# Paced weight loads and a reordered last stretch of a recurrence chain in a two-layer hybrid decoder trunk

## The reference

```python
def token_mixer(h, w_in, ...):
    p = h @ w_in
    p_r, p_m, p_g = jnp.split(p, [RWKV_COLS, RWKV_COLS + MLSTM_COLS], axis=-1)
    y_r = rwkv7_branch(p_r, ...) @ branch_w_rwkv
    y_m = mlstm_branch(p_m, ...) @ branch_w_mlstm
    g_r, g_m = jnp.split(jax.nn.sigmoid(p_g), 2, axis=-1)
    return (g_r * y_r + g_m * y_m) @ w_out

def rwkv7_recurrence(r, w, k, v, a, b):      # per head, state s is 64x64
    def step(s, inp):
        sa = einsum('bhvk,bhk->bhv', s, a_t)
        s = s * w_t + sa * b_t + v_t * k_t
        return s, einsum('bhvk,bhk->bhv', s, r_t)
```

## Time and profile before

| | |
|---|---|
| three runs | 1408.48, 1412.29, 1412.35 us (median 1412.29) |
| the profiled execution's own time | 1416.23 us |
| its span | 1414.5 us |
| TensorE matmul busy | 1383.9 us, 98% of the span |
| mean granted TensorE clock | 0.995 |
| chain of the first layer | about 376 to 453 us from the span's start |
| chain of the second layer | about 1060 to 1140 us |

### The profile page before, as it was taken

The page is one execution under the profiler, slowest core; times in us unless marked ns, Lnnn a source line. Parts: engine busy times, 40 slices in busy tenths (PEclk is TensorE's granted clock), DMA queues, the critical chain, the costliest instruction groups (busy, mean ns, idle before and its releaser), DMA issues.

```text
span 1414.5 us, 31209 instructions
## 1 busy us (share of the span) xinstructions
PE 1383.9 (98%) x13824; PEld 1314.8 (93%) x13824; DVE 1078.2 (76%) x1838; ACT 288.4 (20%) x566; POOL 67.9 (5%) x137
## 2 busy tenths in 40 slices
PE   7999999999999999999999999999998999999998
PEld 3999999888988999999999999988898889999998
DVE  5899889788765769887888886787976575856665
ACT  2211101442231031110031110035231302211101
POOL 5110000000000000100000000000000000000000
PEclk9999999999999999999999999999999999999999
DMA  9999786443423758887768886454442337456530
GB/s 347 323 329 325 285 308 178 141 134 105 115 71 119 238 180 277 278 292 295 254 193 268 280 275 227 157 161 143 120 116 72 116 125 263 134 195 209 191 137 31
DMA packets 214054, 283.16 MB, mean 200 GB/s; under 512 B 13288, under 2 KB 177504, under 8 KB 213920
## 3 DMA queue, kind: packets, MB, share of 16 engines
q1 hardware_dynamic: 194976, 211.11, 46.2%
q0 software_dynamic: 17952, 69.21, 13.8%
q10 hardware_dynamic: 992, 0.85, 0.2%
HBM read 280.10 MB, written 1.05 MB: 199 GB/s over the span
## 4 chain that ended last, share of the span: by engine, by line
PE 94%; DVE 4%; issue 1%; DMA 1%; POOL 0%; ACT 0%; ACTq 0%; POOLq 0%; DVEq 0%
PE ps L1899 92%; PE ps L1903 1%; DMA ada_stage<-in_ada_w_dram 1%; DVE ada_acc L1050 1%; PE ps L2413 0%; DVE ada_turn L1056 0%; DVE ada_red L1057 0%; DVE arena L1279 0%; DVE stat L1332 0%; DVE stat L1326 0%; DVE xn L1329 0%; DVE arena L1330 0%; DVE xn L1339 0%; DVE arena L1282 0%; DVE arena L1280 0%
## 5 line engine op out<-in xcount | busy, mean ns | idle before, releaser
L1899 PE MATMUL ps<-hT,ring 128*128 128x128 f32 (+2 forms) x2352 | 341.9, 302 | 1.7 <-ACT hT L702 1.3
L1899 PEld LDWEIGHTS ps<-hT,ring 128*128 128x128 f32 (+1 forms) x2352 | 313.4, 191 | 26.0 <-issue 8.3
L1899 PE MATMUL ps<-y_both,arena 128*128 128x128 f32 x2304 | 266.6, 275 | 1.0 <-issue 1.0
L1899 PEld LDWEIGHTS ps<-y_both,arena 128*128 128x128 f32 x2304 | 261.8, 192 | 1.5 <-issue 1.5
L1899 PE MATMUL ps<-arena 32*32 32x32 f32 (+6 forms) x4368 | 204.2, 231 | 7.8 <-issue 7.5
L1899 PEld LDWEIGHTS ps<-arena 32*32 32x32 f32 (+3 forms) x4368 | 193.3, 138 | 12.8 <-issue 8.6
L1899 PE MATMUL ps<-arena,ring 128*128 128x128 f32 (+1 forms) x1408 | 199.2, 293 | 0.0
L1899 PEld LDWEIGHTS ps<-arena,ring 128*128 128x128 f32 x1408 | 183.0, 192 | 6.6
L1050 DVE SCALAR_TENSOR_TENSOR ada_acc<-ada_stage,cond,ada_acc 128x1024 f32<-128x1024 f32 (+1 forms) x119 | 149.0, 1252 | 5.4 <-DMA ada_stage<-in_ada_w_dram 1.7
L1899 PE MATMUL ps<-y_both,ring 128*128 128x128 f32 (+1 forms) x1024 | 151.0, 301 | 0.1
L1899 PEld LDWEIGHTS ps<-y_both,ring 128*128 128x128 f32 x1024 | 138.6, 191 | 7.3 <-DVE xn L1803 0.9
(11 more groups left out here) (332 smaller groups left out, 1476.7 us busy)
## 6 DMA issues: line engine op xcount, KB each, us to landing
ring<-in_ffn_w_in_dram SPq DMA_DIRECT2D x86, 1024.0 KB, 7.8
ada_stage<-in_ada_w_dram POOLq DMA_DIRECT2D x66, 1024.0 KB, 5.7
ring<-in_ffn_w_out_dram SPq DMA_DIRECT2D x44, 1024.0 KB, 6.8
ring<-in_mix_w_in_dram SPq DMA_DIRECT2D x46, 512.0 KB, 5.2
ring<-in_mix_w_in_dram SPq DMA_DIRECT2D x12, 1024.0 KB, 5.8
ring<-in_mix_w_in_dram SPq DMA_DIRECT2D x6, 1536.0 KB, 6.5
ring<-in_mix_w_out_dram SPq DMA_DIRECT2D x8, 1024.0 KB, 5.2
arena<-in_ada_w_dram SPq DMA_DIRECT2D x6, 1024.0 KB, 13.7
```

The costliest lines, as they stand in the source:

```text
L1899: return nc.tensor.matmul(out_, lhsT, rhs, start=start, stop=stop, **kw)
```

## The change

Two parts. First, SyncE loads each gate unit and the branch units m0 and m1 in eight pieces of 128 KB. A piece goes to one of three "lanes" (a semaphore each) in turn, and waits for the lane's last piece to have landed; the eighth waits for all three and is the one that counts on `slot_full`. So at most three pieces are in flight. r0 and r1 are still one transfer each. Second, the chain's last products stand in another order.

```diff
-FILL = FFN_FILL + [len(b) for b in PROJ] + [2] * KT + [1] * 4 + [1] * 4 + FFN_FILL
+PIECES, LANES, PACED_BRANCH = 8, 3, 2
+FILL = FFN_FILL + [len(b) for b in PROJ] + [1] * KT + [1] * 4 + [1] * 4 + FFN_FILL
...
+                def piece(n, use, dst, source):
+
+                    if n == PIECES - 1:
+                        for lane, count in zip(lane_full, in_lane):
+                            sp.wait_ge(lane, 16 * count)
+                        sp.dma_start(dst, source).then_inc(full_of(l, use), 16)
+                        return
+                    lane = n % LANES
+                    if n >= LANES:
+                        sp.wait_ge(lane_full[lane], 16 * in_lane[lane])
+                    sp.dma_start(dst, source).then_inc(lane_full[lane], 16)
+                    in_lane[lane] += 1
+
...
-                    for n, col in enumerate((C_GR, C_GM)):
-                        sp.dma_start(view(slot(l, use, 2048), 2, 8, P)[:, n],
-                                     win[:, :, col + ct * P:col + ct * P + P]).then_inc(full_of(l, use), 16)
+                    for n in range(PIECES):
+                        col, k = (C_GR, C_GM)[n % 2] + ct * P, slice(n // 2 * 2, n // 2 * 2 + 2)
+                        piece(n, use, view(slot(l, use, 2048), 2, 8, P)[:, n % 2, k], win[:, k, col:col + P])
...
+                    if n >= PACED_BRANCH:
+                        sp.dma_start(dst, source).then_inc(full_of(l, use), 16)
+                        continue
+                    for i in range(PIECES):
+                        k, part = i // 2, slice(i % 2 * 256, i % 2 * 256 + 256)
+                        piece(i, use, dst[:, k:k + 1, part], source[:, k:k + 1, part])
```

More of the change, by code:

```diff
@@ L416, in trunk @@
         slot_free = sem("slot_free")
+        lane_full = [sem(f"lane_full{n}") for n in range(LANES)]
         ada_full = [sem(f"ada_full{s}") for s in range(2)]
@@ L526, in _ @@
         def _(sp):
+            in_lane = [0] * LANES
             waited = [0]
@@ L585, in _ @@
                         sp.wait_ge(*DV.at(l, "qt"))
-                    sp.dma_start(view(slot(l, use, 2048), 4, 512),
-                                 (branch_m, branch_r)[n // 2][ll, :, cols].rearrange("a (k p) n -> p (a k) n", p=P))\
-                      .then_inc(full_of(l, use), 16)
+                    dst = view(slot(l, use, 2048), 4, 512)
+                    source = (branch_m, branch_r)[n // 2][ll, :, cols].rearrange("a (k p) n -> p (a k) n", p=P)
+                    if n >= PACED_BRANCH:
[4 more added lines that the diff above has]
+                        piece(i, use, dst[:, k:k + 1, part], source[:, k:k + 1, part])
                 for n in range(4):
@@ L2550, in _ @@
                 last.then_inc(*PE.step("h"))
[L2551 to L2555, removed]
                 def state(q, c):
@@ L2574, in _ @@
                 chain_step(1)
[L2575 to L2587, removed]
+                for q, t, h, hh in heads:
+                    i, at = 4 * q + 2 * t + h, (2 * q + t) * 64
+                    for c in range(2):
+                        last = mm(ps[hh, 4 + c, at:at + 64], uz[home(c, h), i, 0:64], mrb[home(c, h), i, :])
@@ new lines, in _, with y_inside @@
+                last.then_inc(*PE.step("qt"))
+                def y_inside():
+                    for q in range(4):
+                        for t in range(TT):
+                            for n in range(2):
+                                for h, hh in enumerate(chunks):
+                                    for c in range(2):
+                                        i, rows, dst = 4 * q + 2 * t + h, home(c, h), y_of(q, t, h)[chunks[c], :]
+                                        if n == 0:
+                                            mm(dst, mrb[rows, i, :], uz[rows, i, 64:128], start=q == t == 0,
+                                               skip_group_check=True)
+                                        else:
+                                            last = mm(dst, mk[rows, i, 64:128], v_tm[rows, q, t, hh], start=False,
+                                                      skip_group_check=True)
+                    last.then_inc(*PE.step("y inside"))
@@ L2588, in _ @@
+                gates("k")
                 pe.wait_ge(*DV.at(l, "chain 1"))
                 chain_step(2)
-                gates("k")
+                pe.wait_ge(*DV.at(l, "qt"))
+                y_inside()
+                pe.wait_ge(*AC.at(l, "low g"))
+                for b in range(2):
+                    for p in (2 * b, 2 * b + 1):
+                        last = mm(duo(b)[:, p % 2, :], up_g[:, p * P:p * P + P], low_g[:, :])
+                    last.then_inc(*PE.step(f"g {b}"))
                 pe.wait_ge(*DV.at(l, "chain 2"))
+                pe.wait_ge(*PE.at(l, "y inside"))
@@ L2597, in _ @@
                 last.then_inc(*PE.step("y"))
[L2599 to L2603, removed]
                 def y_turned(b):
```

## The result

The changed kernel took 1414.57 us in the median of 20 runs (1409.66 to 1417.57), the kernel before 1409.45 us in the median of 20 (1404.90 to 1414.32). The ratio is 1.0034, with a 95% interval of 1.0024 to 1.0044: slower by 5 us, little but outside the interval, where 6.4 us faster were forecast. The profiled execution took 1415.6 us, its span is 1413.9 us. One execution of experiment 1 (3658 us) and one of experiment 3 (5029 us) lie far from all the others and are in no ratio.

The account below looks back on a forecast made before the run. TensorE's matmuls, busy 98% of the span, bound the kernel, so only its stalls could shrink. Terms -7.2 - 1.4 - 1.3 + 0.8 + 2.7 = -6.4 us, from 1412.3 to 1405.9 us; range 1398 to 1416.

Parts of the forecast that it names:

- What an issue stall is: On TensorE: stalls are late instruction fetches, one 16.4 KB packet feeding 254 records, about 127 weight loads.
- gain (a): Burst of m1 and r0 in both chains: pacing gains 8.6 us less 1.4 us of remaining stall, net 7.2 us.
- part 2: New order at the chains' ends: 0.4 us wait in gates k plus 0.94 us at y's copies per chain, 2.7 us lost.
- the burst is only moved: Rival, chance 0.18: r0's burst hits the inside products' block, 3.5 us more a chain, 1412.9 us.
- Gain (b): Stall at 1115.62: m0 no longer comes as 1 MB at once, 1.4 us gained.
- Gain (c): Stalls ending at 402.39 and 1086.87, with the second's clock drop: 1.3 us gained for both, bounds 0 and 4.5.
- Costs of the late gate units: Paced gate units: unit 3 some 2.1 us late for VectorE, gates a 0.4 us later; 0.8 us lost for both layers.
- the floor: Instruction fetch on TensorE: some 4.1 us from one block's start to the next one's readiness, even with idle queues.

Follow-up runs that it names:

- experiment 1: Kernel before with only the new order of the chain's last products, loads as before: 1410.47 us, ratio 0.9985 to the kernel before.
- experiment 3: Kernel before, old order, with only m0 and m1 in eight pieces, gate units in two transfers: 1405.07 us, ratio 0.9943 to the kernel before.
- 5: Changed kernel with r0 also in eight pieces: 1409.33 us, ratio 0.9961 to the kernel before.
- experiment 8: Changed kernel with 236 already-met waits added on TensorE in the first feed-forward half: 1406.33 us, ratio 0.9939 to the kernel before.
- experiment 2: Kernel before with only the paced loads of gate units, m0 and m1, old order: 1403.66 us, ratio 0.9932 to the kernel before.
- experiment 7: Changed kernel with gate units in two transfers again, m0 and m1 still in eight pieces: 1417.81 us, ratio 1.0013 to the kernel before.
- experiment 4: The kernel before, unchanged, run once more for a second profile: 1411.88 us, ratio 0.9997.
- Experiment 9: Old order, gate units 0 to 3 in two transfers, units 4 to 7, m0 and m1 in eight pieces: 1398.49 us, ratio 0.9899 to the kernel before.
- 12: Old order, all gate units, m0 and m1 in eight pieces, run again: 1403.72 us, ratio 0.9944 to the kernel before.

## Why the prediction was wrong

**What an issue stall is: right.** Blocks of some 127 weight loads, delayed by weight traffic. Experiments 3, 5 and 8 show it, each by its own means. The packets say it too: in the kernel before, each stall of over 0.6 us in the two chains ended 2.4 to 2.7 us after a 16 KB instruction packet had begun to move, and ahead of the 3.27 us stall that packet began only at 441.33, as the burst of m1 and r0 ran out. One caution: an "issue" on the weight-load row can be a semaphore that the matmul row names, as the 1.46 us were.

**Part 1, gain (a): right in mechanism, mis-sized by a timetable.** The stalls of m1's and r0's burst went, with their half clock (experiment 2: 160 loads uncut in the first chain, 0.55 us left of 2.19 in the second). But I gave 0.7 us a chain for r0's burst on the next block, and it was 2.04 and 1.79. The term behind it was the time of r0's issue: I put 441.6 and it was 443.57, because m1's pieces started 1 us later, landed after 2.6 us and not 2.3, over three rounds, and r0 followed the eighth of them after 0.4 us. The burst thus ended near 448.4, 0.3 us before the old block ran out at 448.69.

**The step that failed: the two idle times of the chain's end were priced apart.** My text has "0.7 us of stall remain in each chain" under (a) and "the idle time is 1.34 + 0.07 = 1.4 us" under part 2, with "y 446.6 to 447.7" between them. The block's edge lay five loads ahead of y's end, so they were one idle stretch of 3.6 and 3.4 us, and the clock fell: 1.7 and 3.1 us on the first branch products. My sum had nothing for the clock there; only the rival "the burst is only moved" had one, at 1.5 us a chain and a chance of 0.18, and it came nearest to what happened. By the profile: stalls 3.8 and half clock 4.8 us, where my sum had 1.4. That is 7.2 us, more than the whole forecast gain.

The mean granted clock, which is on record for every execution, points the same way, though it does not say where in the program the clock was lost. A thousandth of it is 1.4 us. It is 0.9936 over the changed kernel's 20 executions and 0.9929 in experiment 7, which has the same chain end; it is 0.9955 for the kernel before (experiment 4), 0.9964 for the order alone, 0.9974 for the paced loads alone and 0.9975 with the edge moved.

**The terms together, between the two profiled executions.** The chains' ends: 3.0 us lost, where I had 4.5 gained (7.2 less 2.7). Gain (b): 1.6 for 1.4. Gain (c): 4.5 for 1.3. Costs of the late gate units: 2.4 for 0.8. That makes 0.7 us gained for 6.4, and the two executions are 0.6 apart.

**Part 2 alone: nearly right.** TensorE's wait in gates k was 0.23 us and not 0.4, that for y's copies 1.60 and not 1.4. By itself the new order is no loss (experiment 1: 0.9985), because it also breaks up the 160 small weight loads that the burst cut in two. I had put that gain into (a), as if it were pacing's. The two parts remove the same stall, so their gains do not add, and only their costs do.

**Gain (c) and the floor: wrong, to my favour.** Stalls of 1.92 and 2.04 us became 0.48 and 0.51 (experiment 2: 0.27 and none), with the half clock of the second; 4.5 us, my upper bound, where I took 1.3. Some of it comes back one block later: 0.81 us at 406.57 in experiment 2, 0.44 us in the changed kernel's second chain. The 4.1 us "floor" was not a floor. It was two parts in a row: from the stall's end at 379.79 to the start of the next packet 1.45 us, and from there to the end of the next stall 2.63 us. Behind other stalls of the kernel before the first part is shorter (1.05 us at 443.87), and in the changed kernel packets begin 3.3 us apart (400.99, 404.32, 407.75). Why the first part was 1.45 us there stays open.

**Gain (b), 1.4 us: there by the number, not shown as pacing's.** The changed kernel has no stall there, and nor has the second profile of the kernel before, with m0 in one transfer (experiment 4). It comes and goes.

**Costs of part 1: right place, too small.** I had gates a 0.4 us later. It began 1.0 us later in the first chain, largely at half clock, and ended 2.3 us later; in the second chain 0.1 us. The delay at VectorE was nearly as forecast (2.6 us for 2.1, of which 1.7 vanish in gaps, as I had it). It does not come at one place, though: TensorE waits 1.67 us for the transposition and 1.46 us for `gate_pair(2)`, in place of the stalls of 1.23 and 0.66 us that were there before, and the missing term is again the half clock behind two waits that lie close together. Experiment 9 against 12 prices the early units' pieces at 5.2 us in all.

**The median of before: a second mistake, of 5.7 us.** My terms are differences to one execution, and it lay 6.8 us over the median of 20, while the changed kernel's profiled execution is 1.0 us over its own. So the profiles differ by -0.6 us and the medians by +5.1. Two of my gains stood on what that execution had beyond the usual: 1.5 us of half clock in the second chain under (a), and (b). The second profile of the kernel before has neither. The forecast for part 1 alone would have been -9.1 us, and experiment 2 measured 0.9932, 8.4 to 9.6 us; with (c) 3.2 us too small and 2.9 us counted that the kernel before does not always lose, this agreement is in part luck.

## What to carry to other kernels

Idle times of TensorE cannot be priced one by one. Look at where each new wait lies next to every other, and at what they add up to: here 1.6 us alone left the clock full, 2.04 and 1.60 us side by side were followed by half clock, and that cost as much as the stalls. Take the gains from more than one profile of the kernel before: what a single execution lost beyond the usual is no gain of the change. In dense stretches of small products a list of instructions has edges like a tile has: count about 127 float32 weight loads from one late block to the next, and see what transfer is in flight while the next one is fetched. When TensorE waits for "issue", look at the matmul row too before you call it an instruction fetch. And when two edits cure the same stall, measure each alone; here one was worth 0.7%, the other next to nothing, and both together cost 0.3%.

## What the runs showed that I had not expected

236 instructions that do nothing made the kernel 8 us faster by the medians (experiment 8), by moving the edges of the instruction blocks. The same stall, 2.19 and 2.20 us in two executions of one kernel, was followed by half clock in the one and full clock in the other; a stall of 1.92 us was not followed by it in the kernel before and was in experiment 3 (0.50 granted from 402 to 404), 3.27 was both times. That is one source of this kernel's spread of 10 us; another lies in its first 20 us, where two executions of one kernel parted by 1.8 us. And a 1 MB unit in eight pieces, three in flight, took 7.8 us to its last issue and about 10 us to land, against 5.8, and the chain ran faster for it: what counts here is not the time of the load but what it keeps waiting.
